# Sums and roots of ten norms with the tokens on partitions, spread back by matmuls into PSUM

## What is computed

```python
def rms_norm(x, g):                       # first layer
    xf = x.astype(jnp.float32)
    y = xf * lax.rsqrt(jnp.mean(xf * xf, axis=-1, keepdims=True) + EPS)
    return (y * g.astype(jnp.float32)).astype(x.dtype)

def modulate(x, g, shift, scale):         # second and third layer
    return rmsnorm(x, g) * (1 + scale) + shift

        h = rms_norm(x, attn_pre_norm[layer])          # n1
        h = hybrid_mixer(h, ...)
        x = x + rms_norm(h, attn_post_norm[layer])     # n2
        h = rms_norm(x, ffn_pre_norm[layer])           # n3
        h = conv_ffn(h, ...)
        x = x + rms_norm(h, ffn_post_norm[layer])      # n4
```

## Time and profile before

| | us |
|---|---|
| median of 3 runs | 3108.38 (3108.37 to 3108.43) |
| span of the profiled execution | 3106.6 |
| PE matmuls busy | 2993.9 (96%) |
| DVE busy | 1293.0 (42%) |
| ACT busy | 799.4 (26%) |
| POOL busy | 731.4 (24%) |
| weights and other data read from HBM | 362.30 MB, 117 GB/s over the span |

### The profile page before, as it was taken

One profiled execution on the slowest core, in us unless ns is written; L12 is line 12 of the kernel. 1 busy time (PEld: TensorE's weight loads), 2 busy tenths in 40 slices (PEclk: granted clock), 3 DMA queues, 4 the chain that ended last, 5 costly groups with the idle time before them and its releaser, 6 DMA issues.

```text
span 3106.6 us, 36995 instructions
## 1 busy us (share of the span) xinstructions
PE 2993.9 (96%) x14508; PEld 2260.7 (73%) x14508; DVE 1293.0 (42%) x2448; ACT 799.4 (26%) x1735; POOL 731.4 (24%) x664
## 2 busy tenths in 40 slices
PE   8999999998999999999999999999999999999998
PEld 7766788887865545555548688888776766678897
DVE  1244232213146554655553343342336555541652
ACT  1012121111013315555530021010103355540210
POOL 0000110002420002222133324434230111110686
PEclk9999999999999899999999999999999999999999
DMA  6455334442336222322212212222321333334443
GB/s 242 159 205 215 111 132 149 149 151 95 113 124 236 82 97 95 106 84 97 107 68 82 82 68 82 95 82 95 102 102 55 103 107 104 109 109 151 148 164 108
DMA packets 65191, 369.92 MB, mean 119 GB/s; under 512 B 6074, under 2 KB 21498, under 8 KB 22672
## 3 DMA queue, kind: packets, MB, share of 16 engines
q1 hardware_dynamic: 48768, 334.60, 30.1%
q10 hardware_dynamic: 15296, 29.56, 3.0%
q0 software_dynamic: 976, 3.63, 0.3%
HBM read 362.30 MB, written 1.28 MB: 117 GB/s over the span
## 4 chain that ended last, share of the span: by engine, by line
PE 92%; DVE 5%; ACT 2%; issue 1%; DMA 0%; POOL 0%; DVEq 0%; POOLq 0%; ACTq 0%
PE PB L1226 13%; PE PB L468 13%; PE PA L468 8%; PE PB L350 8%; PE PB L1086 7%; PE PS L468 6%; PE PB L979 6%; PE PB L1207 6%; PE PB L394 5%; PE PB L1240 3%; PE PA L1309 2%; PE PB L568 2%; PE PA L1278 1%; PE PA L1292 1%; PE PA L568 1%; PE PB L372 1%
## 5 line engine op out<-in xcount | busy, mean ns | idle before, releaser
L1226 PE MATMUL PB<-H,ring 128*128 128x512 f32 (+1 forms) x1024 | 429.6, 568 | 0.0
L1226 PEld LDWEIGHTS PB<-H,ring 128*128 128x128 f32 x1024 | 192.6, 191 | 185.9 <-issue 180.5
L503 POOL TENSOR_TENSOR sums<-ring 128x512 f32<-128x512 f32 x84 | 108.6, 1293 | 498.7 <-PE PA L468 252.9
L1086 PE MATMUL PB<-H,ring 128*128 128x256 f32 x992 | 214.3, 379 | 0.0
L1086 PEld LDWEIGHTS PB<-H,ring 128*128 128x128 f32 x992 | 188.5, 190 | 25.6
L468 PE MATMUL PB<-work,sums 128*128 128x256 f32 (+1 forms) x1104 | 200.6, 339 | 0.0
L2334 DVE SCALAR_TENSOR_TENSOR work<-PB,par,work 128x510 f32<-128x510 f32 (+3 forms) x256 | 181.6, 713 | 24.1 <-ACT work L1698 17.3
L468 PEld LDWEIGHTS PB<-work,sums 128*128 128x128 f32 x1104 | 177.8, 191 | 17.6
L2680 POOL TENSOR_TENSOR work<-work 128x256 f32<-128x256 f32 x96 | 59.7, 643 | 517.8 <-ACT work L1720 415.8
L979 PE MATMUL PB<-H,ring 128*128 128x256 f32 (+1 forms) x640 | 177.7, 432 | 1.5 <-ACT mod L1476 0.9
L1207 PE MATMUL PB<-H,ring 128*128 128x512 f32 (+1 forms) x512 | 175.5, 493 | 0.0
(11 more groups left out here) (349 smaller groups left out, 5026.2 us busy)
## 6 DMA issues: line engine op xcount, KB each, us to landing
ring<-stream SPq DMA_DIRECT2D x315, 1024.0 KB, 4.8
sums<-cs_rows ACTq DMA_DIRECT2D x16, 1024.0 KB, 4.7
sums<-cs_rows ACTq DMA_DIRECT2D x16, 512.0 KB, 3.9
work<-work ACTq DMA_DIRECT2D x16, 256.0 KB, 4.6
work<-scratch POOLq DMA_DIRECT2D x1, 2560.0 KB, 16.6
X<-xT SPq DMA_DIRECT2D x2, 1024.0 KB, 13.2
out<-H SPq DMA_DIRECT2D x1, 1024.0 KB, 4.8
con<-consts SPq DMA_DIRECT2D x1, 652.0 KB, 18.2
```

The source lines that it names most:

```text
L503: nc.gpsimd.tensor_tensor(su[:, 0], a21, a22, ALU.add).then_inc(sem("w_summed"), 1)
L1086: mm = pe.matmul(PB[:, pair, t, 0:T1], ring[:, c % SLOTS, k, t * P:(t + 1) * P], h1(k), start=(k == 0), stop=(k == KT - 1))
L1226: mm = pe.matmul(PB[:, pair, t, 0:Tc], ring[:, c % SLOTS, k, t * P:(t + 1) * P], H[:, k, 0:Tc], start=(k == 0), stop=(k == KT - 1))
```

## The change

The norms' sums change sides. Now the squared tile is the stationary operand, 128 tokens of it at a time, and a single column that holds 1/1024 is the moving one: a matmul gives one column with 128 tokens on the partitions. Two such columns (four for 512 tokens) hold all sums. ACT's root and DVE's reciprocal work on 128x2 or 128x4 in `ROOT`. To bring the roots back to the columns, PE multiplies: the stationary operand is a column of `ROOT`, broadcast to 128x128, the moving one the identity; 128 tokens for each matmul, into the bank that also held the sums (`norm_spread`). DVE reads the roots there (`root_of`). For n2, n3 and n4 a second pair of matmuls writes the same into `PS`, and ACT copies it to `RSTD`, which POOL and L2145 still read. `n3`, `m10c` and `m10` use `PA1`.

DVE's products of `residual1` go to PSUM (five half banks, `tiles`), and its sums read them there. `X_ORDER` changes. The identity is loaded early, in a DMA of its own, and the reciprocals of m20 and m11 for the second 256 columns are gone. Where PE makes the spreads is written by hand: for m10c behind group 2 of `down`, for n3 and n4 in the middle of a row of matmuls, elsewhere right behind the sums.

```diff
-        ROOTED = ["n1", "n2", "n3", "m10c", "n4", "m10", "m20", "m20b", "m11", "m11b", "m21", "final"]
+        COPIED = ["n2", "n3", "n4"]
...
-            return PA[1] if tag == "m10c" else PA[0]
+            return PA[1] if tag in ("n3", "m10c", "m10") else PA[0]
+
+        def root_of(tag):
+
+            return sums_to(tag)[:, 0:TT if tag in ("m20", "m11") else T1]
...
-                mm = pe.matmul(sums_to(tag)[:, 0:T], full(ONE_D), sq(k), start=(i == 0), stop=(i == KT - 1))
+                for t in range(T // P):
+                    mm = pe.matmul(sums_to(tag)[:, t:t + 1], sq(k)[:, t * P:(t + 1) * P], ONE_D,
+                                   start=(i == 0 and t == 0), stop=(i == KT - 1), skip_group_check=True)
...
+        ROOT = small[:, 96:100]
+
+        def norm_root(act, tag):
+
+            n = root_of(tag).shape[-1] // P
             act.wait_ge(sem("norm_sum"), SUMMED.index(tag) + 1)
-            nc.scalar.activation(RSTD[:, col:col + T1], sums_to(tag)[:, half * T1:half * T1 + T1], ACT.Sqrt, bias=EPS_C)\
-                .then_inc(sem("norm_root"), 1)
-
-        def norm_rstd(v, step, col=0):
-
-            v.wait_ge(sem("norm_root"), ROOTED.index(step) + 1)
-            nc.vector.reciprocal(RSTD[:, col:col + T1], RSTD[:, col:col + T1]).then_inc(sem("norm_rstd"), 1)
-            v.wait_ge(sem("norm_rstd"), ROOTED.index(step) + 1)
+            nc.scalar.activation(ROOT[:, 0:n], sums_to(tag)[:, 0:n], ACT.Sqrt, bias=EPS_C).then_inc(sem("norm_root"), 1)
+            if tag in COPIED:
+                act.wait_ge(sem("norm_spread_twice"), COPIED.index(tag) + 1)
+                nc.scalar.activation(RSTD[:, 0:T1], PS[:, 1, 0:T1], ACT.Copy).then_inc(sem("norm_copied"), 1)
+
+        def norm_rstd(v, tag):
+
+            n = root_of(tag).shape[-1] // P
+            v.wait_ge(sem("norm_root"), SUMMED.index(tag) + 1)
+            nc.vector.reciprocal(ROOT[:, 0:n], ROOT[:, 0:n]).then_inc(sem("norm_inverse"), 1)
+            v.wait_ge(sem("norm_spread"), SUMMED.index(tag) + 1)
+
+        def norm_spread(pe, tag):
+
+            n = root_of(tag).shape[-1] // P
+            pe.wait_ge(sem("norm_inverse"), SUMMED.index(tag) + 1)
+            for t in range(n):
+                mm = pe.matmul(sums_to(tag)[:, t * P:(t + 1) * P], full(ROOT[:, t:t + 1]), ident, start=True, stop=True)
+            mm.then_inc(sem("norm_spread"), 1)
+            if tag in COPIED:
+                for t in range(n):
+                    mm = pe.matmul(PS[:, 1, t * P:(t + 1) * P], full(ROOT[:, t:t + 1]), ident, start=True, stop=True)
+                mm.then_inc(sem("norm_spread_twice"), 1)
...
-        X_ORDER = (0, 5, 1, 6, 2, 3, 7, 4)
+        X_ORDER = (0, 1, 5, 2, 3, 6, 4, 7)
...
+            sp.dma_start(con[:, 0:P], consts[:, 0:P]).then_inc(loaded, 16)
...
-            sp.dma_start(con[:, :], consts).then_inc(loaded_late, 16)
+            sp.dma_start(con[:, P:N_CONSTS], consts[:, P:N_CONSTS]).then_inc(loaded_late, 16)
...
+            pe.wait_ge(loaded, 16 * 2)
+            norm_spread(pe, "n1")
...
                         norm_added(pe, tag, T1, lambda k: SQ[:, k, 0:T1])
+                        if tag != "n4":
+                            norm_spread(pe, tag)
                     if j == 1 and tag == "n4":
                         norm_added(pe, "m10c", T1, lambda k: SQ[:, k, T1:TT])
+                    if j == 2 and tag == "n4":
+                        norm_spread(pe, "m10c")
...
+                    elif i == 4:
+                        norm_spread(pe, "n3")
...
+                        if n == 0 and k == 4:
+                            norm_spread(pe, "n4")
                         if n == 1 and k == 0:
                             norm_sums(pe, "m10", T1, lambda k: SQ[:, k, 0:T1], X_ORDER)
+                            norm_spread(pe, "m10")
...
+                    norm_spread(pe, "m11")
+                    pe_features(pe, "q1", hl, T, ready=lambda k: shifted("m11")(0, k),
+                                after=lambda j: pe.wait_ge(sem("mod_scaled"), past("m11") + 2 * KT))
...
+                free = 1 - GROUPS["up" if tag == "n2" else "q0n"][0][0]
+                tiles = [bank[:, T1 * i:T1 * i + T1] for bank in (PS[:, 0], PB[:, free, 0], PB[:, free, 1]) for i in range(2)]
                 for i in range(len(DVE_TILES) + 1):
                     if i < len(DVE_TILES):
                         k = DVE_TILES[i]
-                        vec.tensor_tensor(src[:, k, :], src[:, k, :], RSTD[:, 0:T1], ALU.mult)\
-                            .then_inc(sem(f"{tag}_part"), 1)
+                        vec.tensor_tensor(tiles[i], src[:, k, :], root_of(tag), ALU.mult).then_inc(sem(f"{tag}_part"), 1)
                     if i:
                         k = DVE_TILES[i - 1]
                         v.wait_ge(sem(f"{tag}_part"), i)
-                        vec.tensor_tensor(x1(k), x1(k), src[:, k, :], ALU.add).then_inc(sem(f"{tag}_x_dve"), 1)
+                        vec.tensor_tensor(x1(k), x1(k), tiles[i - 1], ALU.add).then_inc(sem(f"{tag}_x_dve"), 1)
...
-            def norm_mod(la, step, part, s_):
+            def norm_mod(la, tag, part, s_, at=0):
 
 
                 cols = slice(s_ * T1, (s_ + 1) * T1)
-                norm_rstd(v, step, s_ * T1)
+                if not at:
+                    norm_rstd(v, tag)
                 for k in range(KT):
-                    vec.scalar_tensor_tensor(H[:, k, cols], X[:, k, cols], mod_(la, part, k, s_), RSTD[:, cols],
-                                             ALU.mult, ALU.mult).then_inc(sem("mod_scaled"), 1)
+                    vec.scalar_tensor_tensor(H[:, k, cols], X[:, k, cols], mod_(la, part, k, s_),
+                                             root_of(tag)[:, at:at + T1], ALU.mult, ALU.mult).then_inc(sem("mod_scaled"), 1)
...
-                pool.wait_ge(sem("norm_rstd"), ROOTED.index(tag) + 1)
+                pool.wait_ge(sem("norm_copied"), COPIED.index(tag) + 1)
```

More of the change, by code:

```diff
@@ L1612, in _ @@
                 else:
-                    for half in range(2):
-                        norm_root(act, "m11", "m11", half, half * T1)
+                    norm_root(act, "m11")
                     shift(1, "m11", 0, (0, 1))
@@ L1854, in _ @@
                     x_squares("m20", SQ_OUT, 3)
-                    for half in range(2):
-                        norm_root(act, "m20", "m20", half, half * T1)
+                    norm_root(act, "m20")
                     shift(0, "m20", 3, (0, 1))
```

40 lines of the change are left out of this document (21 added, 19 removed).

## The result

The changed kernel took 3111.47 us (median of 20 runs, 3109.80 to 3115.56) where the kernel before took 3108.34 (20 runs, 3097.15 to 3111.39). The ratio of the runs is 1.0020, 95% interval 1.0012 to 1.0028: slower by 3 us in the medians, at the edge of the 0.2% that the prediction called no change, and more than the measurement is uncertain. The profiled execution took 3115.38 us, with a span of 3113.2.

What follows compares the result with a forecast made beforehand. TensorE, busy 96% of the span, was taken to bound the kernel. The terms at the norms sum to +0.3 us; 3106.6 (profiled span) + 0.3 + 1.8 (median over span) = 3108.7 us, range 3101.0 to 3114.0.

Steps and rivals of the forecast that it cites:

- m10c: Before `down`'s fourth group, the late spread holds DVE and ACT: +5.3, then clock +2.0; +7.3 us (5.3 to 8.6).
- the charge for the clock: At the norms, the clock stays low for 4.0 us after PE resumes, costing half, 2.0 us.
- n1: At the kernel's first norm, chain -0.8 and +0.4 for a clock that may rise later: -0.4 us (-0.8 to +0.2).
- The choice on the clock: At the norms, one-column sums are as good as a gap, so the clock falls, staying low 4.0 us after PE resumes.
- Rival 1: At n3, m10, m11 and m21, one-column sums hold the clock: -8.5 us in all, 3100.2 us; chance 0.13.
- rival 3: At `down`, the m10c spread holds nobody: without the 7.3 us the time is 3101.4 us; chance 0.05.
- Rival 2: At six resumptions after norms, the clock stays low for 6.5 us: +7.5 us, giving 3116.2 us; chance 0.08.
- n2 and n3: At these norms before `up`, -1.4 so far, then +2.0 for the clock falling in n3's sums: +0.6 us (-1.9 to +2.6).
- n4 and m10: Around `q0n`, earlier sums and a shorter chain let PE go on at 757.7, not 762.1: -4.4 us (-7.1 to -2.8).
- m21: At this norm and its projection, chain -1.2, contention -0.1, low clock +0.7, faster records: -1.7 us (-4.5 to -0.6).
- m20, m11, final: At these three norms, small changes in sums, chain and clock: -0.6, +0.4 and -0.9 us.

Runs made afterwards that it cites:

- E1: The changed kernel with the m10c spread issued behind the first chunk of `down`'s third group instead of its last; 3106.08 us, ratio 0.9997.
- E2: The changed kernel with the moving operand of all norm sums 128 columns wide instead of one; 3103.77 us, ratio 0.9988.
- E8: The kernel before the change, with the dt projection's matmuls moving 128 columns instead of 64, the second 64 unread; 3102.10 us, ratio 0.9992.
- E10: E3 plus unread matmuls in PE's waits at m20, m11, m21 and final, and the dt projection widened to 128 columns; 3081.52 us, ratio 0.9933.
- E11: The kernel before the change, with the dt projection widened as in E8 and unread matmuls in its own waits at m20, m11, m21 and final; 3088.58 us, ratio 0.9958.
- E3: The changed kernel with both the earlier m10c spread of E1 and the 128-column sums of E2; 3096.88 us, ratio 0.9964.

## Why the prediction was wrong

The sum came to +0.3 and 3108.7 us, no change that can be told. The measured 3111.5 lies inside the range, but the change is slower, by more than the measurement is uncertain. The step that failed is the charge for the clock. The prediction took it as 4.0 us at the low level behind each resumption (2.0 us of time), put +0.4 at n1 and nothing at n4. Three things went beyond that, and all of them cost: the one-column sums of n1 and the projection behind them, the fall in the middle of n3's sums, and the fall behind n4's. With the smaller misses they add to some 9 us. That the time came out only 3 us off is luck: 4.8 us came back at the dt projection, which no term had.

**m10c** (+7.3, measured +8.2): the mechanism, its place and the wait were right (4.63 us and a spread of 0.61 against 5.3); E1 removed it. The term for the clock was too small: 4.0 us of low clock, 2.0, where it was low for 5.9 us after PE had resumed (717.5 to 723.4), 2.9.

**The choice on the clock** was right in kind: the granted clock is 0.50 behind n3's sums, as named beforehand, and E2 turned it to 1.00 by the width alone. Rival 1 falls, and rival 3 with m10c. The 4.0 us itself was fair, if a little short, where PE had stopped: after it resumed, the clock stayed low for 5.9 us at m10c, 4.6 at m10, 5.5 at m20, 4.0 at m11 and 3.4 at m21. Rival 2 wanted 6.0 or more at each, so its condition was not met there. Its 3116.2 is the right direction, and near what the time would be without the dt projection's 4.8, but for other reasons. What was wrong is that only the time behind a gap was charged: over and behind one-column sums the clock was low where PE had no gap to resume from.

**n2 and n3** (+0.6, measured +2.4): at n3 the clock was low through 6.8 us of unbroken work, 3.3 us in place of 2.0: 4.68 us for the sums in place of 3.74, 1.9 us more on the eight records behind, and 0.5 on the spread. At n2 it was low for 5.2 us after PE resumed, where it was 3.0 before; that was in no term.

**n1** (-0.4, measured +1.2, and 2.5 of the +3.9 behind it) is the term that failed worst. I took the kernel's first sums for a stretch where the clock is low in any case. Before, it rose within them; with one column it didn't, and it stayed low into the projection. Besides, the bias matmul now between sums and spread (0.7 us of delay) was not in the sum, though the diff shows its place.

**n4 and m10** (-4.4, measured -3.2) and **m21** (-1.7, measured -2.8): right in sign and within their bounds; at m10 PE resumed 2.95 us after the end of its sums (763.61 to 766.56), as named, and the reciprocals took 0.17. What n4 lacks is its own stretch of low clock, 3.4 us or 1.7 us of time. (The prediction lets q0 begin at 762.1; the earlier trace rows has 762.33. It changes little.) m21's gain was larger since its projection got 8 products in 3.22 us in place of 4.43, and the clock was low for 3.4 us after PE resumed where it was 6.5 before. The products before:

```profile
2883.85 4.43 DVE L2187 SCALAR_TENSOR_TENSOR H<-X,mod,rstd 128x256 f32<-128x256 f32 x8
```

**m20, m11, final**: within 1 us each.

**The -4.8 between q0 and m20's sums** is not in any term. I had the row of 13.92 us before me and used it as a price; I did not see that the same group could take half in another execution of the same code. E8 shows what it hangs on; why all traces of the changed kernel met it with the clock up stays open.

## What to carry to other kernels

A matmul with one column took as long here as one with 128 (0.117 us a record at full clock): give it 128, since here the clock fell at n3 and stayed low at n1 with one-column sums, and did neither with wide ones. Look for a step that the change puts behind a long uninterruptible stretch of work, and for whoever stands in order behind it: the m10c spread cost 8 us for 0.6 us of matmuls. And before shortening a chain in which PE waits, try filling the wait with matmuls that nobody reads. Here that was worth 11.8 us, and the change itself, with its two mends and the waits filled on both sides, 7.1 (E10 against E11).

## What the hardware showed that was not expected

- Sixty-four records of 64 columns, issued without a pause, took 13.92 us or 7.36 us by the level of the clock at their start, in kernels with the same code there; with 128 columns it took 9.78 in the one trace that began at the low level, and 7.41 in the three that began at full clock.
- The Trainium skill ("TensorE: Matmul & The Clock Gate", "What's actually happening") says that the clock is low by default and that activity releases it. The traces agree for wide matmuls: in E3 the clock rose within the first 32 records. They don't for the changed kernel's n1, where PE was busy for 6.95 us without a pause and still at 0.2175 us a record.
- In the changed kernel the granted clock of the windows reads 1.00 from the first matmul to 28 us, while the records of the sums take the price of 1.2 GHz: before its first change the column is not to be trusted.
- The runs of one unchanged kernel lie between 3097 and 3111 us, and the mean granted clock goes with the time, from 0.988 in the fastest to 0.981 in the slowest.
